# Expert stages on groups of 32 tokens, the last expert added by one-hot products, token sums on TensorE, and two norms in one

## The reference

```python
def rmsnorm(x, g):
    xf = x.astype(jnp.float32)
    y = xf * lax.rsqrt(jnp.mean(xf * xf, axis=-1, keepdims=True) + EPS)
    return (y * g.astype(jnp.float32)).astype(x.dtype)

def expert_choice_ffn(h, router, w_gate, w_up, w_down):
    bn, t, _ = h.shape
    cap = CAPACITY_FACTOR * t // N_EXPERTS          # 64 latent tokens, 32 context tokens
    aff = jax.nn.softmax(h.astype(jnp.float32) @ router.astype(jnp.float32), axis=-1)
    gate, idx = lax.top_k(jnp.swapaxes(aff, 1, 2), cap)
    bidx = jnp.arange(bn)[:, None, None]
    xs = h[bidx, idx]
    hid = jax.nn.silu(jnp.einsum('becd,edf->becf', xs, w_gate)) * jnp.einsum('becd,edf->becf', xs, w_up)
    y = jnp.einsum('becf,efd->becd', hid, w_down) * gate[..., None].astype(h.dtype)
    return jnp.zeros_like(h).at[bidx, idx].add(y)
```

## Time and profile before

| | us |
|---|---|
| median of 3 runs | 3123.28 (3120.75 to 3128.16) |
| the profiled execution's own time | 3124.46 |
| its span in the trace | 3122.7 |
| TensorE busy (matmul) | 2579.2, 83% of the span |
| VectorE, ScalarE, GpSimd busy | 1148.7, 457.5, 242.8 |
| ring chunks `moe_ring<-in_experts` | 384 of 1024 KB, median 21.8 from issue to landing |
| all DMA | 603.60 MB, mean 193 GB/s |

### The profile page before, as it was taken

How to read it: one execution, slowest core, us unless ns; L and a number is a source line. 1 busy time by engine, 2 the same in 40 slices (tenths; PEclk the granted TensorE clock), 3 DMA queues, 4 the chain that set the end, 5 groups by cost and what they waited for, 6 DMA issues and landing times. The chain is left out here.

```text
span 3122.7 us, 33638 instructions
## 1 busy us (share of the span) xinstructions
PE 2579.2 (83%) x13966; PEld 1540.1 (49%) x13966; DVE 1148.7 (37%) x1937; ACT 457.5 (15%) x932; POOL 242.8 (8%) x208
## 2 busy tenths in 40 slices
PE   4999879299999994999787687777748766799999
PEld 2585665144444432578435222222237534688888
DVE  3635674500000004227675300000053666534551
ACT  2101441200000002000241100000010221111000
POOL 1000001001111102002001000000021200100000
PEclk8999879699999996999898799999969866899999
DMA  6331312689999964435002899999822100122221
GB/s 241 142 122 66 93 61 95 253 343 388 389 396 396 390 271 140 148 126 151 26 0 109 323 397 396 402 403 394 347 95 96 45 12 1 68 81 88 98 81 58
DMA packets 97959, 603.60 MB, mean 193 GB/s; under 512 B 12408, under 2 KB 15816, under 8 KB 32656
## 3 DMA queue, kind: packets, MB, share of 16 engines
q1 hardware_dynamic: 85024, 572.96, 47.1%
q0 software_dynamic: 11632, 26.39, 3.8%
q10 hardware_dynamic: 1152, 2.10, 0.2%
HBM read 574.03 MB, written 23.18 MB: 191 GB/s over the span
## 5 line engine op out<-in xcount | busy, mean ns | idle before, releaser
L1021 PE MATMUL moe_psg<-moe_ring,moe_xs 128*64 128x512 f32 x1024 | 253.6, 636 | 41.4 <-DMA moe_ring<-in_experts 39.2
L1021 PE MATMUL moe_psd<-moe_ring,moe_hid_t 128*64 128x512 f32 x1024 | 237.3, 602 | 30.1 <-DMA moe_ring<-in_experts 28.5
L1183 DVE TENSOR_SCALAR moe_y_l<-moe_psd,moe_gates 128x512 f32<-128x512 f32 x32 | 24.0, 751 | 644.9 <-PE moe_psh L1035 331.5
L1021 PE MATMUL moe_psu<-moe_ring,moe_xs 128*64 128x512 f32 x1024 | 235.8, 599 | 30.3 <-DMA moe_ring<-in_experts 30.1
L1021 PEld LDWEIGHTS moe_psg<-moe_ring,moe_xs 128*64 128x64 f32 x1024 | 72.6, 144 | 192.3 <-issue 163.1
L1021 PEld LDWEIGHTS moe_psd<-moe_ring,moe_hid_t 128*64 128x64 f32 x1024 | 68.7, 137 | 190.0 <-issue 129.3
L1175 DVE TENSOR_TENSOR moe_hid_l<-moe_silu_l,moe_psu 128x512 f32<-128x512 f32 x32 | 22.0, 688 | 365.8 <-PE moe_psgu L1035 189.8
L1021 PEld LDWEIGHTS moe_psu<-moe_ring,moe_xs 128*64 128x64 f32 x1024 | 67.1, 136 | 177.1 <-issue 110.9
L1084 POOL DMA_INDIRECT acc_lat<-moe_y_l,moe_rows_id x32 | 50.1, 1564 | 915.3 <-DVE moe_y_c L1185 464.6
L1035 PE MATMUL moe_psgu<-moe_ring,moe_xs 128*32 128x256 f32 x2048 | 117.1, 380 | 0.0
L1035 PEld LDWEIGHTS moe_psgu<-moe_ring,moe_xs 128*32 128x32 f32 x2048 | 63.3, 110 | 64.4 <-issue 26.0
(11 more groups left out here) (645 smaller groups left out, 4278.0 us busy)
## 6 DMA issues: line engine op xcount, KB each, us to landing
moe_ring<-in_experts SPq DMA_DIRECT2D x384, 1024.0 KB, 21.8
feed_f_slots<-in_ffn_gate SPq DMA_DIRECT2D x11, 1024.0 KB, 4.9
feed_f_slots<-in_ffn_up SPq DMA_DIRECT2D x11, 1024.0 KB, 4.8
feed_f_slots<-in_ffn_down SPq DMA_DIRECT2D x8, 1408.0 KB, 6.0
mod_ada_w<-in_ada_w SPq DMA_DIRECT2D x2, 4096.0 KB, 13.4
qk_ada_w<-in_ada_w SPq DMA_DIRECT2D x8, 1024.0 KB, 4.8
gate_rows<-in_ada_w SPq DMA_DIRECT2D x8, 1024.0 KB, 5.4
mout_ada_w<-in_ada_w SPq DMA_DIRECT2D x8, 1024.0 KB, 4.8
```

The lines of the kernel that those rows point to most:

```text
L1021: mm = pe.matmul(ps_lat[part][64 * half:64 * half + 64, :], lhs, ring[:, n % SLOTS, m, half * HALF:(half + 1) * HALF], start=(k == 0), sto ...
L1183: ins = dve.tensor_scalar(y_l[:], ps_lat[DOWN][:], gates[:, 0, e, :], None, ALU.mult)
```

## The change

- Every token row is split into quarters of 256 features, and the slots of an expert into groups of 32 tokens: two groups for the latents, a third for the context in layer 0. Partition 32 q + j of a group holds quarter q of token j. One accumulator `acc` and one `h_rows` hold all tokens as rows of 1 KB. The gathers and additions are one indirect DMA of 128 rows of 1 KB per group.
- VectorE turns rows and hidden values with its transposition of 32x32 blocks (`dve.transpose`); the weights' rows are reordered on the host to fit. TensorE's turns and ScalarE's copies go.
- One `product` per part works through the chunks once, group by group in four column quarters, and frees each chunk when it is done with it.
- The last expert's output is not sent to DRAM. SP loads the accumulator after the additions of expert 14. TensorE turns it by products with ident into PSUM and adds the last expert by a product of y (32 tokens of a quarter) with a one-hot matrix that holds the gate at the token's column. This stands in the same block as the experts.
- The squares are summed over the features by TensorE with a two-column weight into `K.total`, per token (column 1 of layer 1 weighs with the square of the final gain).
- Norms take the root and the reciprocal of one value per token, spread it with diag(1/rms) through a ones product, and scale from PSUM. Where `given` is not set, `K.sumsq` is summed over the partitions first by small products. The norms nf and n2a are one stage, `double_norm`; x itself is scaled on VectorE beside the first product stage of the hybrid block (`finish_x`).

The core of the diff:

```diff
-        rstd = ctx.enter_context(nc.sbuf_tensor(f"{name}_rstd", [P, TOK], F32))
...
-                for a, b in segments:
-                    mm = pe.matmul(ps[:, a:b], K.ones[:], K.sumsq[:, a:b], start=True, stop=True)
+                if not given:
+                    for t in range(tiles):
+                        mm = pe.matmul(ps_c[:, t:t + 1], K.sumsq[:, t * P:(t + 1) * P], K.ones[:, 0:1], start=True, stop=True)
+                    mm.then_inc(sig["summed"], 1)
+                pe.wait_ge(sig["diag"], 1)
+                for a, b in segments:
+                    mm = pe.matmul(ps[:, a:b], K.ones[:], diag[:].rearrange("p t i -> p (t i)")[:, a:b], start=True, stop=True)
+                mm.then_inc(sig["spread"], 1)
...
+def double_norm(nc, K, name, once, prefetch):
...
+            @block.scalar
+            def _(act):
+                act.activation(r[:], K.total[:, 0:LT, 0], ACT.Sqrt, bias=K.col("eps"), scale=1.0 / D).then_inc(sig["root"], 1)
+                act.wait_ge(sig["mean"], 1)
+                act.activation(s[:], mean[:], ACT.Sqrt, bias=K.col("eps"), scale=1.0 / D).then_inc(sig["root"], 1)
+                act.wait_ge(sig["spread"], 2)
+                act.activation(once[:], ps[:, 1], ACT.Copy)
...
+                step(dve.tensor_tensor(mean[:], K.total[:, 0:LT, 1], r[:], ALU.mult))
+                dve.tensor_tensor(mean[:], mean[:], r[:], ALU.mult).then_inc(sig["mean"], 1)
+                dve.wait_ge(sig["root"], 2)
+                step(dve.reciprocal(s[:], s[:]))
+                step(dve.tensor_tensor(s[:], s[:], r[:], ALU.mult))
+                dve.tensor_tensor(diag[:, 0], *spread_of(s), ALU.mult).then_inc(sig["diag"], 1)
+                dve.tensor_tensor(diag[:, 1], *spread_of(r), ALU.mult).then_inc(sig["diag"], 1)
...
+            def product(pe, e, part):
+                for c in range(4):
+                    n = first_chunk[e, part] + c
+                    pe.wait_ge(landed[n % SLOTS], 16 * (n // SLOTS + 1))
+                    for m in range(2):
+                        k = 2 * c + m
+                        for g in range(G):
+                            turned = hid_t[:, g] if part == DOWN else xs[:, e % 2, g]
+                            for q in range(4):
+                                mm = pe.matmul(group_ps(part, g)[32 * q:32 * q + 32], turned[:, k * GROUP:(k + 1) * GROUP],
+                                               ring[:, n % SLOTS, m, q * QUARTER:(q + 1) * QUARTER],
+                                               start=(k == 0 and g != 1), stop=(k == KT - 1), skip_group_check=True)
                     mm.then_inc(sig["w_used"], 1)
...
+                    sp.wait_ge(sig["added"], 16 * G * LAST)
+                    sp.dma_start(acc_tok, acc.rearrange("(t p a) c -> p t (a c)", p=P, a=4)).then_inc(sig["sum_landed"], 16)
...
                     def gather(e):
+                        for g in range(G):
+                            pool.indirect_dma_start(out=rows[:, g], out_offset=None, in_=h_rows,
+                                                    in_offset=bass.IndirectOffsetOnAxis(rows_id[:, g, e:e + 1], 0)
+                                                    ).then_inc(sig["gathered"], 16)
...
+                            for tt in range(t0, t1):
+                                pe.matmul(ps[:, bank(u), (tt - t0) * P:(tt - t0 + 1) * P], acc_tok[:, tt, dt * P:(dt + 1) * P],
+                                          K.ident[:], start=(tt == t0), stop=False, skip_group_check=True)
...
+                        for g in groups:
+                            for u in batch:
+                                dt = units[u][1]
+                                quad = slice(32 * (dt // 2), 32 * (dt // 2) + 32)
+                                mm = pe.matmul(ps[:, bank(u), 0:span(u)], y[quad, g, (dt % 2) * P:(dt % 2 + 1) * P],
+                                               onehot[quad, g, 0:span(u)], start=False, stop=(g == groups[-1]),
+                                               skip_group_check=True)
...
+                            for tt in range(t0, t1):
+                                mm = pe.matmul(ps[:, 7, 2 * tt:2 * tt + 2], sq[:, u % 8, (tt - t0) * P:(tt - t0 + 1) * P],
+                                               weigh[:, dt], start=(u == 0 and tt == 0), stop=(dt == KT - 1),
+                                               skip_group_check=True)
...
+                    def turn_rows(e):
+                        dve.wait_ge(sig["gathered"], 16 * G * (e + 1))
+                        if e >= 2:
+                            dve.wait_ge(sig["w_used"], used_up(e - 2, UP))
+                        dve.transpose(xs[:, e % 2].rearrange("p g c -> p (g c)"),
+                                      rows[:].rearrange("p g c -> p (g c)")).then_inc(sig["xs"], 1)
...
+                        dve.transpose(hid_t[:].rearrange("p g c -> p (g c)"),
+                                      hid[:].rearrange("p g c -> p (g c)")).then_inc(sig["hid_t"], 1)
...
+        def finish_x(dve, sig, c):
+            for k in (c + 1,) if c else (0, 1):
+                dve.scalar_tensor_tensor(K.x[:, k, 0:LAT], K.x[:, k, 0:LAT], K.col("final_g", k), once[:], ALU.mult, ALU.mult)
```

More of the change, by code:

```diff
@@ L743, in _ @@
                             act.activation(out[:, k, a:b], out[:, k, a:b], ACT.Identity, bias=shift(r, k))
-                if again:
-                    squares(act, sig)
-            if again:
-                @block.gpsimd
-                def _(pool):
-                    pool.wait_ge(sig["summed"], 1)
-                    sums(pool, sig)
             @block.vector
@@ L1018, in lat_pass @@
                         k = 2 * c + m
-                        for half in range(2):
-                            lhs = xs[:, e % 2, k, 0:64] if part != DOWN else hid_t[:, k % 4, 64 * (k // 4):64 * (k // 4) + 64]
-                            mm = pe.matmul(ps_lat[part][64 * half:64 * half + 64, :], lhs,
-                                           ring[:, n % SLOTS, m, half * HALF:(half + 1) * HALF],
-                                           start=(k == 0), stop=(k == KT - 1))
-                    if not both:
-                        mm.then_inc(sig["w_used"], 1)
@@ L1081, in add_up @@
                         if e >= 1:
[L1082 to L1085 removed]
+                            pool.wait_ge(sig["added"], 16 * G * e)
@@ L1092, in _ @@
                         if e >= 1:
                             add_up(e - 1)
-                    add_up(EXPERTS - 1)
-                    pool.wait_ge(sig["added"], 16 * EXPERTS * len(streams))
+                    add_up(LAST - 1)
                 @block.tensor
                 def _(pe):
-                    turn_rows(pe, 0)
                     pe.wait_ge(sig["xs"], 1)
-                    lat_pass(pe, 0, GATE, range(4))
-                    if both:
-                        ctx_pass(pe, 0, GATE)
+                    product(pe, 0, GATE)
@@ L1104, in _ @@
                     for e in range(EXPERTS):
[L1105 to L1107 removed]
                         if e >= 1:
                             pe.wait_ge(sig["hid"], e)
[L1110 to L1125 removed]
+                        product(pe, e, UP)
@@ new lines, in _ @@
+                    dve.memset(weigh[:], 1.0).then_inc(sig["weigh"], 1)
+                    if not both:
+                        dve.wait_ge(sig["weigh"], 1)
+                        dve.tensor_tensor(weigh[:, :, 1], K.cols("final_g", KT), K.cols("final_g", KT),
+                                          ALU.mult).then_inc(sig["weigh"], 1)
+                    dve.wait_ge(sig["count"], 16)
+                    for g in range(G):
+                        dve.tensor_scalar(onehot[:, g], count[:], last_place[:, g, :], gates[:, g, LAST, :], ALU.is_equal,
+                                          ALU.mult).then_inc(sig["onehot"], 1)
```

361 lines of the change are left out of this document (178 added, 183 removed).

## The result

The changed kernel took 3050.46 us (median of 4 runs, 3044.54 to 3057.38) against 3124.16 for the kernel before in the same session (4 runs, 3120.75 to 3128.16): ratio 0.9769, 95% interval 0.9748 to 0.979, 74 us less. The forecast was 3067, range 3040 to 3100. The profiled execution took 3047.25 us with a span of 3045.5, 77.2 less than the span before. A later repetition of the same kernel gave 3056.11, ratio 0.9784 (0.9763 to 0.9804), so the size is 67 to 74 us. One execution of that repetition (3118.94 us, at a mean granted clock of 0.88 where the others have 0.92) is in a slower state and is left out of its median, as are two of the kernel before beside it.

What follows compares the result with a forecast made beforehand. DMA was taken to bound layer 1 and TensorE, only just, layer 0, with nothing overlapping at the ends of the expert stages. Terms summed to -56.4 us from 3124.46: 3068.1, as a median 3066.9, said as 3067; range 3040 to 3100.

Steps and rivals of the forecast that it cites:

- Layer 1's experts: Layer 1's start gains 1.5 us from no fill and shorter lists; the experts' pace is taken as unchanged.
- the two corrections: Layer 1, 1 KB packets: gather priced by bytes 1.2 us less, additions priced by packet 1.2 more; taken as no change.
- Rival (a): Gather gets cheap over all partitions: up to 1.2 us x 15 in layer 1, 5 to 15 in layer 0; 3037, chance 0.17.
- (b): Additions in both layers cost by the packet: 15 x (1.2 + 1.7) = +43 us, 3110; chance 0.11.
- Layer 0's experts: DMA binds at 34.5 us an expert and the chunk stream starts earlier; experts end at 1143.4 instead of 1167.7, -24.3 us.
- +3.5 in all: Start of layer 0's experts: a larger gather instruction and two more gathers ahead of the first product cost 3.5 us.
- The accumulators: Wait for the accumulator's load after the last expert product shrinks: -14.6 us in layer 0, -14.4 in layer 1.
- The sums: Accumulator turns, one-hot products and two-column records on TensorE: 32.3 us in layer 0 (+11.7), 22.5 in layer 1 (+9.1).
- rival (c): TensorE runs at half clock in both layers' sums after idling before them: +30 us, 3097; chance 0.10.
- The norms: Layer 1's end: nf and n2a as one norm take 14.2 us against 33.4, -19.1; n1a after layer 0 gains 2.0.
- (d): Slower: gathers have a fixed price per piece, +207 us, 3274; per DMA at most +90, 3157; chance 0.06.
- (e): Column-tiled records run slower over a whole part, so TensorE still binds layer 0 at 33.8 us: +15, 3082; chance 0.06.

Runs made afterwards that it cites:

- the first four experiments: One session, each against the changed kernel: no gathers 3026.94, no additions 3003.68, the old gather 3081.11, layer 0's chunks freed only in a second pass 3057.1 us.
- all eight later runs: Two later sessions: changed kernel repeated (3056.11 us) and seven variants of last expert, squares, norms, turning records or layer 1's additions, 3029.08 to 3075.64 us.

## Why the prediction was right, and where it was off

The sign and the bound of each stage held; the sum was 21 us too small by the profiled executions (17 by the medians), 19.7 of it in the two stretches of the experts. Of that, 2.4 are the norms n0b and n1b, which the forecast had in its term for the other norms.

- **Layer 1's experts** (forecast -1.5, measured -13.1, of which n1b's norm is 0.7). The step that failed is "I take no change: the two corrections are of like size and of opposite sign". They are opposite, but the gather gave 1.33 us and the addition took 0.50. The gather went all the way to my lower bound, its price by bytes (0.63 against 0.62), the addition less than half of the way to its upper one (0.5 of 1.2). Rival (a) had the mechanism with the right size for layer 1 (1.2 us) and was held to 0.17; (b) was real and small. The measured 3050 lies between the forecast's 3067 and (a)'s 3037, and the range holds it because (a) had set its lower end.
- **Layer 0's experts** (-24.3, measured -32.4). DMA binds as foreseen and the stream starts 5.0 us after the first product, as written (5.4). The first product came at 616.6, not 620.7: 2.2 us were gained before the router's product (n0b's norm 1.7, and 0.5 ahead of it), and the step "+3.5 in all" for two more gathers failed. From the first gather's issue to the turn it is 5.47 us (610.11 to 615.58) where one gather took 4.42: they cost 1.05, since each lands beside the next one's issue. From the stream's start to the last product it is 513.2 us against 517.3 forecast, and 529.3 with the old gather in the same kernel. Without the 1.7 of its longer last product the new gather saves 14.4 us, 1.0 an expert. On the other side the kernel with the old gather, whose DMA work was to be that of the forecast, took some 10 us more than the forecast. The dearer additions are one candidate (0.50 x 1.5 = 0.75 an expert, an estimate from layer 1). The end of the stream is another: I let it run full up to the last chunk, but the DMA share is 0.51 in 1120 to 1130. No run separates them.
- **The accumulators** (-14.6 and -14.4; -14.1 and -14.0): right. Putting the last expert back shows it in full for layer 0 and for 11.2 of 14.0 us in layer 1.
- **The sums.** Layer 1: 22.2 against 22.5, in part by luck: the 64 two-column records took 10.36 us, 0.162 each as forecast, but as a mixture of full clock up to 2225 and 0.51 behind it. Layer 0: 35.6 against 32.3, and the terms inside were off both ways: turns 16.4 for 12.5, one-hot products 6.0 for 4.4, two-column records 12.1 for 15.4. The clock is rival (c) in part. In the table of stretches above the granted clock is 0.68 right behind the wait, 1.00 (the level of 2.4 GHz) through the first turns and one-hot products, and 0.50 (1.2 GHz) in 1165 to 1170, behind two groups of two-column records. The two-column records make turns behind them half as fast, always behind the second group and at times behind the first; without them 16 turns keep 2.05 us. The first 32 turns took 5.18 us behind the wait instead of 3.84, but 3.84 to 6.52 in the other runs behind waits of 3.3 to 5.1 us, so what decides this 1.3 us isn't shown.
- Two-column records, full clock: 3.73 us for 32, 0.117 each; half clock: 6.99, 0.218. I had taken 0.16 from rows with 64 moving columns between other products, in a stretch with a mean granted clock of 0.68 to 0.74 (their weight loads took 191 ns). The Trainium skill, page TensorE: Matmul & The Clock Gate, section LDWEIGHTS (loading the stationary operand), has 107 ns for 128 columns: near the trace's 117 ns at full clock, and about half of its 218 ns at the half clock.
- **The norms** (-19.1, measured -20.5; n1a -2.0, -3.1): right; scaling from PSUM, taken as +0.9, costs nothing (8.49 us for sixteen instructions at n1a, 8.55 before). `finish_x` shows as forecast: from its first product to that of the next stage, the first product stage of the hybrid block takes 96.9 us (2245.05 to 2341.97) instead of 96.2 (2319.40 to 2415.61), +0.7, and the last of its scalings (2332.80, 0.74 us) stands behind all other work of the stage.
- **(d)**, a price per piece or per DMA that makes it slower: refuted. 256 pieces of 1 KB in two DMAs cost 0.63 us, less than 64 of 4 KB in one. The Trainium skill's 2 us fixed per DMA from GpSimd (page DMA: Bandwidth & Descriptors, section Anatomy of one DMA — SWDGE (gpsimd) path) isn't time taken from the stream; by that reading layer 1's additions would cost 4 us, and they cost 1.5. **(e)**: refuted, TensorE's pace is 31.1 us an expert, and 32.0 in the last two sessions, not 33.8.

## What to carry to other kernels

Price a gather by its shape before its bytes: pieces of 1 KB on all 128 partitions cost their bytes, rows of 4 KB on 64 three times as much. When two corrections of opposite sign are both bounded only from afar, keep them as two terms with ranges of their own, not as one of size zero. Where a stage is bound by DMA and TensorE has time left, sums kept in SBUF by one-hot products were cheaper than additions in DRAM (18.8 us in layer 1), and here a record with two moving columns costs as much as one with 128 (0.117 us against 0.120), plus the clock that the records behind it can lose.

## What was not expected of the hardware

- 64 rows of 4 KB cost 1.96 us of the stream, 256 pieces of 1 KB on all partitions 0.63. Whether the number of partitions or the length of the pieces does it, no run here separates.
- A float32 transposition into PSUM followed by products with `start` off gives the whole sum, if only the first tile of the bank sets `start`. With `start` on every tile part of the sum is missing. The Trainium skill, page PSUM — Partial Sum Buffer, section The four PSUM rules, says that a starting product clears the marks of the whole bank, and that a product without `start` then overwrites where the mark is clear; the two runs agree.
- The same kernel had a TensorE pace of 31.08 us an expert in one session and 32.03 in another, at a granted clock of 1.00 in both. It goes by the session or the chip and not by the kernel: the first four experiments have 31.08 wherever TensorE doesn't wait, all eight later runs about 32.0.
